# First attention stage of a two-block transformer on one core: compression branch threaded through the attention steps, twelve modulation steps moved beside weight panels, mask and score products in half-array pairs

## What is computed

```python
mod = jax.nn.silu(c) @ ada_w[i] + ada_b[i]            # six modulation vectors of 1024
h = rms_norm(x, attn_norm[i]) * (1.0 + sc_a) + sh_a
mq, mk, mv, nq, nkv, ng = jnp.split(h @ w_in, SPARSE_SPLITS, axis=-1)
o_moba = moba_attention(qk_prep(mq...), qk_prep(mk...), mv)
kc = nsa_compress(qk_prep(kv[0, 0]...), cmp_pos[0], cmp_w1[0], cmp_w2[0])
vc = nsa_compress(kv[0, 1], cmp_pos[1], cmp_w1[1], cmp_w2[1])
...
blocks = t[:, :, idx] + pos_emb                       # 15 blocks of 32 tokens, stride 16
hid = jax.nn.silu(jnp.einsum('bgnld,lde->bgne', blocks, w1))
return jnp.einsum('bgne,ed->bgnd', hid, w2)
...
o = g[..., 0:1] * o_c + g[..., 1:2] * o_s + g[..., 2:3] * o_w
```

## Time and profile before

| what | us |
|---|---|
| median of 3 runs | 1750.68 |
| the profiled execution, first to last instruction | 1748.3 |
| PE busy in it | 1575.0 (90%) |
| DVE busy | 940.4 (54%) |
| ACT busy | 718.2 (41%) |
| the three input panels, 45.4 to 112.9 | 67.5 |
| from the last panel to the first attention step, 112.9 to 197.6 | 84.6 |
| `attention(0)`, 197.6 to 261.0 | 63.4 |

### The profile page before, as it was taken

One profiled execution on the slowest core, in us unless ns is written; L12 is line 12 of the kernel. 1 busy time (PEld: TensorE's weight loads), 2 busy tenths in 40 slices (PEclk: granted clock), 3 DMA queues, 4 the chain that ended last, 5 costly groups with the idle time before them and its releaser, 6 DMA issues.

```text
span 1748.3 us, 24466 instructions
## 1 busy us (share of the span) xinstructions
PE 1575.0 (90%) x10302; PEld 1322.1 (76%) x10302; DVE 940.4 (54%) x1610; ACT 718.2 (41%) x1098; POOL 0.2 (0%) x4
## 2 busy tenths in 40 slices
PE   3966988999989888999988999889999795999997
PEld 1753677999868657999768998679987673779986
DVE  2591346434577776433566345663355786364455
ACT  1441244334445434333335554354544443345543
POOL 0000000000000000000000000000000000000000
PEclk9988798999989889999988999889999897989999
DMA  9844602985545546998753645549755353436452
GB/s 359 313 149 158 224 19 79 315 286 188 174 147 185 176 142 214 307 307 302 242 180 97 190 172 193 181 137 300 249 185 202 109 181 109 162 129 192 169 192 85
DMA packets 165845, 336.42 MB, mean 192 GB/s; under 512 B 8160, under 2 KB 109160, under 8 KB 165480
## 3 DMA queue, kind: packets, MB, share of 16 engines
q1 hardware_dynamic: 134720, 226.71, 38.0%
q10 hardware_dynamic: 31016, 108.16, 18.2%
HBM read 333.79 MB, written 1.05 MB: 192 GB/s over the span
## 4 chain that ended last, share of the span: by engine, by line
PE 80%; DVE 13%; DMA 2%; ACT 2%; issue 1%; ACTq 0%; SPq 0%; DVEq 0%
PE ps L1508 21%; PE ps L1509 21%; PE ps L1510 20%; PE ps L1480 5%; DVE wlo L903 3%; PE ps L1639 2%; DVE res L981 1%; DVE work L979 1%; PE ps L1636 1%; PE ps L1723 1%; PE ps L1673 1%; PE ps L1706 1%; DMA ring<-in_ada_w_dram 1%; PE ps L1702 1%; DVE work L1066 1%
## 5 line engine op out<-in xcount | busy, mean ns | idle before, releaser
L903 DVE TENSOR_TENSOR wlo<-wraw,whi 128x1024 fp32r<-128x1024 f32 (+1 forms) x424 | 497.9, 1216 | 404.4 <-ACT whi L526 403.9
L526 ACT ACTIVATE whi<-wraw 128x1024 fp32r<-128x1024 f32 (+1 forms) x424 | 423.1, 1045 | 468.7 <-PE ps L1510 447.0
L1508 PE MATMUL ps<-hT_hi,whi 128*128 128x256 f32 x1472 | 422.5, 287 | 0.0
L1509 PE MATMUL ps<-hT_lo,whi 128*128 128x256 f32 x1472 | 416.9, 283 | 0.0
L1510 PE MATMUL ps<-hT_hi,wlo 128*128 128x256 f32 x1472 | 416.5, 283 | 0.0
L1508 PEld LDWEIGHTS ps<-hT_hi,whi 128*128 128x128 f32 x1472 | 282.7, 192 | 20.3 <-issue 18.1
L1509 PEld LDWEIGHTS ps<-hT_lo,whi 128*128 128x128 f32 x1472 | 282.9, 192 | 0.0
L1510 PEld LDWEIGHTS ps<-hT_hi,wlo 128*128 128x128 f32 x1472 | 282.8, 192 | 0.0
L1508 PE MATMUL ps<-whi,act_hi 128*128 128x512 f32 x560 | 219.0, 391 | 0.0
L1509 PE MATMUL ps<-wlo,act_hi 128*128 128x512 f32 x560 | 218.1, 390 | 0.0
L1510 PE MATMUL ps<-whi,act_lo 128*128 128x512 f32 x560 | 217.9, 389 | 0.0
(11 more groups left out here) (200 smaller groups left out, 1372.1 us busy)
## 6 DMA issues: line engine op xcount, KB each, us to landing
wraw<-in_mlp_w_dram SPq DMA_DIRECT2D x96, 1024.0 KB, 5.3
ring<-in_ada_w_dram ACTq DMA_DIRECT2D x90, 1024.0 KB, 5.3
wraw<-in_ffn_w_gate_dram SPq DMA_DIRECT2D x22, 1024.0 KB, 6.4
wraw<-in_ffn_w_up_dram SPq DMA_DIRECT2D x22, 1024.0 KB, 5.6
wraw<-in_ffn_w_down_dram SPq DMA_DIRECT2D x22, 1024.0 KB, 4.9
wraw<-in_diff_w_in_dram SPq DMA_DIRECT2D x12, 1024.0 KB, 4.9
wraw<-in_attn_w_qkv_dram SPq DMA_DIRECT2D x12, 1024.0 KB, 5.1
wraw<-in_sp_w_in_dram SPq DMA_DIRECT2D x8, 1024.0 KB, 13.0
```

The lines of the kernel that those rows point to most:

```text
L526: nc.scalar.activation(whi[:, u % 2, part], wraw[:, u % 4, part], ACT.Copy).then_inc(hi_ready, 1)
L903: nc.vector.tensor_tensor(wlo[:, u % 2, part], wraw[:, u % 4, part], whi[:, u % 2, part].bitcast(F32), ALU.subtract).then_inc(lo_ready, 1)
L1508: mm(dst, s_hi, m_hi, start=start, stop=False, skip_group_check=skip)
L1509: mm(dst, s_hi, m_lo, start=False, stop=False, skip_group_check=skip)
```

## The change

- The panels are computed in the order `in0_2`, `in0_0`, `in0_1` (`IN0_ORDER`), each with `ada_step` beside all its units; `attention(0)` has no modulation steps now (`a.ada` 0) and `out0` has four. Norm and rotation of the NSA keys run beside `in0_0`, of the MoBA heads beside `in0_1`, of the NSA queries between the groups of `turns`. `turns(0)` is in parts, the groups with the compression keys first.
- The four units of `w1` leave the ring and pass through `wraw` between `in0_1` and `out0` (`compression_dma`); `out0`'s units wait for `cmp_used`. The first `w1` product alternates between its two column groups.
- The rest of the compression branch is placed in iterations 0 to 12 of `attention(0)` (`compression(i)` on PE, ACT and DVE), all of it in PSUM bank 7. The compressed rows are added instead of copied, and the first NSA heads write instead of adding.
- The splits of `out0`'s first two units are done in iterations 8 and 10 of `attention(0)`.
- `scores` in stages 0 and 1: the mask is two products of 64 rows per head, and the two heads alternate, instruction by instruction.
- `columns(0, 1)` comes after `out0`; on DVE it follows `residual`. The load of `ctx` moves from before `in0_1` to the eighth unit of `up0`.

```diff
-        for n, (a, b) in enumerate(((0, 1024), (1024, 2048), (2048, SP_IN))):
+        IN0_ORDER = (2, 0, 1)
+        IN0_SPAN = ((0, 1024), (1024, 2048), (2048, SP_IN))
+        for n in IN0_ORDER:
+            a, b = IN0_SPAN[n]
...
-            a.ada = {0: 4, 1: 8, 3: 8}[stage]
+            a.ada = {0: 0, 1: 8, 3: 8}[stage]
...
+            def compression_dma(j):
+                before = CMP_RAW + j - 4
+                sp.wait_ge(lo_ready, 2 * (before + 1))
+                slot = (CMP_RAW + j) % 4
+                dst = wraw[:, slot, :].rearrange("p (k e) -> p k e", k=8)
+                sp.dma_start(dst, w1c[j % 2][:, (j // 2) * 8:(j // 2 + 1) * 8, :]).then_inc(raw_full[slot], 16)
...
+            row_segment("in0_1", ada=True, heads=lambda i: heads0(0, (i,)), own=True)
+            nc.vector.memset(mark[:, 1:2], 0.0).then_inc(sem("moba_heads0"), 1)
+            panel_rows(r0, 1024, 1024)
+            turns(0, 0, 4)
...
+            nc.vector.memset(hidr[:, :], 0.0).then_inc(sem("hidr_zero"), 1)
+            nc.vector.memset(cmp_s, NEG)
+            heads0(1, (0, 1))
+            turns(0, 4, 6)
+            heads0(1, (2,))
+            turns(0, 6, 8)
+            heads0(1, (3,))
+            nc.vector.memset(mark[:, 1:2], 0.0).then_inc(sem("query_heads0"), 1)
...
+                if i == 3:
+                    dve.wait_ge(sem("cmp_vrep"), 1)
+                    nc.vector.tensor_tensor(vbd, ps[:, LINK_BANK, :], const("headmask"), ALU.mult).then_inc(sem("cmp_vbd"), 1)
...
+                if i in (10, 12):
+                    t = (i - 10) // 2
+                    dve.wait_ge(sem("cmp_pv"), t + 1)
+                    compressed_rows(t)
+                if i in (8, 10):
+                    split_unit(by_name["out0"]["base"] + (i - 8) // 2)
...
-                        mm(ps[:, bank, 0:256], ident_r[:, :], causal_r[:, :], start=True, stop=False, skip_group_check=True)
-                        mm(ps[:, bank, 0:128], q[:, 0:128], k[:, 0:128], start=False, stop=True, skip_group_check=True)
...
+                        for half in range(2):
+                            for m in range(2):
+                                lo, hi = HD * m, HD * m + HD
+                                bank = 2 * (i % 2) + m
+                                mm(ps[:, bank, 0:256], half_r[lo:hi, HD - HD * half:3 * HD - HD * half], causal_r[lo:hi, half, :, :].rearrange("p b n -> p (b n)"),
+                                   start=(half == 0), stop=False, skip_group_check=True)
+                        for tq, tk, at in ((0, 0, 0), (1, 1, 128), (1, 0, 256)):
+                            for m in range(2):
+                                q, k, _ = operands(i, m)
+                                bank = 2 * (i % 2) + m
+                                ins = mm(ps[:, bank, at:at + P], q[:, tq * P:(tq + 1) * P], k[:, tk * P:(tk + 1) * P], start=False, stop=True, skip_group_check=True)
...
-            ada_step()
-            pe.wait_ge(sem("cmp_silu"), 1)
...
+            attention(0, beside=compression)
+            pe.wait_ge(sem("cmp_taken"), 2)
+            out_turn(0)
+            row_segment("out0", ada=True)
             columns(0, 1, 6)
```

More of the change, by code:

```diff
@@ L1323, in _ @@
+            attention(0, beside=compression)
+            out_turn(0)
+            row_segment("out0", ada=True)
+            residual(0)
             columns(0, 1)
[L1324 to L1326 removed]
             norm()
@@ L1665, in gate, with turns @@
                     gate_out[0] = (gate_copied, 2 * sum(1 for g in GATES[:e + 1] if not (g[0] == 2 and g[2] == 0)))
-            def turns(stage):
-                for g, (srcs, _) in enumerate(q_groups(stage)):
+            def turns(stage, first=0, last=None):
+                groups = q_groups(stage)
+                last = len(groups) if last is None else last
+                for g in range(first, last):
+                    srcs, _ = groups[g]
                     if g >= 4:
```

453 lines of the change are left out of this document (245 added, 208 removed).

## The result

The changed kernel takes 1711.58 us (median of 4 runs, 1709.14 to 1715.86), the kernel before, run beside it, 1752.41. The ratio is 0.977, 95% interval 0.975 to 0.979. The forecast was 1702 with a range of 1690 to 1714. The profiled execution took 1709.3 us. Its span is 1707.2, against the span of 1748.3 from which the sum was made: -41.1 where the sum said -48.8. So the median is in the range and 9.6 us above the forecast, and one of the four executions, at 1715.86, is above the range. 7.7 of the 9.6 us are in the sum; the other 2 are that the median lies 4.4 above this span, where the forecast added 2.4. The 7.7 are not spread over the terms. They sit in one place, C, and A gives a part back.

A forecast was written before the change was run, and what follows sets the result against it. PE was taken to bound panels and attention, with no engine full in the 84.6 us between. Terms +9.2 - 63.0 + 2.6 - 1.1 + 5.0 - 1.5 = -48.8 on 1748.3 give 1699.5; median 2.4 above, 1702; range 1690 to 1714.

The forecast's parts named there:

- C: Attention stage: cheaper scores, added branch work and waits give 66.0 us against 63.4: +2.6, bounds -5 to +12.
- A: Panels: eight more modulation steps beside them, less a shorter first split and a wait: +9.2 us, bounds +8 to +14.
- B: Last panel to first attention step: the serial branch goes, DVE sets 21.6 us of 84.6: -63.0, bounds -64 to -58.
- plus 1.5 for a cold start: Attention stage: 1.5 us added to 64.5 for beginning at the low clock, giving 66.0.
- If the clock falls to the low level in mid attention: Attention stage: listed sign of a wrong forecast; it would double the 3.2 us of a step.
- D: Behind attention: the four `modrow` transposes move into PE's wait behind `out0`: -1.1 us.
- E: `out0`: it gets the four modulation steps that attention gave up: +5.0 us.
- F: `attention(1)`: DVE is the bound, so cheaper scores give at most 1.9 us; taken as -1.5.
- R1: Attention scores: loads of two row groups do not overlap: 1706 us, 1710 with the `w1` product serial too; chance 0.20.
- R2: Attention stage: the branch's links and two splits hold it longer than laid out: 1708 to 1720 us; chance 0.13.
- R3: Attention stage: the waits of 17.8 us overlap better, the stage takes 57: 1692 us; chance 0.04.
- R4: Scores: each row-group change drains the array; gain gone from 0.29 us a change, 1762 us at 0.35; chance 0.02.

The follow-up runs named there:

- e5_serial_w1: Changed kernel with the `w1` product going through its two column groups one after the other instead of alternating; 1708.0 us.
- e10_all_narrow: Changed kernel with `out0`'s splits late, `vcr` spread by wide products, and filler transposes nobody reads in PE's attention-stage waits; 1694.1 us.
- e9_pause_in_before: Kernel before the change, with PE made to wait once, in iteration 6 of `attention(0)`, for six extra DVE subtractions; 1776.0 us against 1751.2.
- e12_tail: e10_all_narrow plus filler transposes in its last two pauses, before the last values and before `out_turn`; 1689.4 us.
- e1_fill: Changed kernel with filler transposes nobody reads in front of PE's waits for copied probabilities, `vcr` and `vbd`; 1704.0 us against 1711.6.
- e4_by_head: Changed kernel with the scores of the two heads done one after the other instead of alternating, in both attention stages; 1723.5 us.
- e2_no_branch: Changed kernel with the compression branch left out of the attention stage, so the result lacks compressed attention; 1694.3 us.
- e8_by_head_no_branch: Changed kernel with the edits of e2_no_branch and e4_by_head together; 1706.5 us.
- e11_all_broad: Same as e10_all_narrow, but with one product of 256 columns as filler in place of each four transposes; 1695.0 us.

## Why the forecast was right, and what was off in it

- **A** was too dear by 3.7 us. The price of a step beside a unit held (6.68 and 5.53 us a period). The first split was put at -0.5; in fact the panels started 3.4 us earlier, about 2.8 of them the load that landed sooner and 0.7 the shorter split. The load rate of the narrow panel was put too high: its unit is 792 of 1024 columns, 0.81 MB, so with the ring unit 1.86 MB in 5.7 us are 326 GB/s and not 368, and no load stopped PE there.
- **B** held: 20.9 against 21.6, with DVE as the bound and the `w1` product beside it. The overlap of the column groups, taken from the modulation step, is shown by e5_serial_w1.
- **C** is the term that was mis-sized: +14.6 for +2.6. Not in the scores (1.10 us at the high level against 1.35), not in the waits (16.1 against 18.6), and not in the count of PE's work, which e10_all_narrow gives as 45.6 against 45.9. The step that failed is "plus 1.5 for a cold start". The forecast listed waits of 17.8 us in all, and costed each at its own length. The clock fell behind most of them and stayed low longer than they were: the scores behind the wait of 1.47 us and behind that of 2.85 still run at the low level. 61.9 us busy against 45.9 at the high level are 16.0 that this cost; 1.5 of them were foreseen, and the waits came out 2.5 shorter, which leaves the 12.0. "If the clock falls to the low level in mid attention" stood under what would prove the forecast wrong, without a price and without a chance. e9_pause_in_before shows such a price: 6 us of pause, 18 us behind it. That the low level is the loss is shown by that run and by e10_all_narrow. That pauses alone bring it about is shown for the 6 us pause and for the two at the end (e12_tail); for the links of the branch it is not, by the second fall in e1_fill.
- **D**: `columns` did move off the path, but `out_turn` got 0.8 us longer at the low level, so nothing shows at its old place; 0.8 us came back between `out0` and `up0`. **E**: +5.7 for +5.0, its first step cold, 1.94 instead of 1.07. **F** held.
- **R1** fell. Two row groups do load side by side: 0.063 us an instruction alternating, 0.84/7 = 0.12 one head at a time, both high. At the low level it is 0.12 alternating (1.41 us from 164.84 to 166.25 for 12) and 1.65/8 = 0.21 one at a time. So in one row group the price of an instruction with its load nearly doubles when the clock halves. The Trainium skill, page "TensorE: Matmul & The Clock Gate", section "LDWEIGHTS (loading the stationary operand)", gives a load its columns over 1.2 GHz and names no dependence on the clock; the low rows, and those of the earlier trace rows, disagree, and the measurement decides.
- **R2** named the right place with the wrong mechanism. The two splits cost 2.85 and 3.03 us of waiting, as laid out; moving them brought 7.5 us, since PE's busy time fell by 4.2 in the stage beside 2.1 of waiting. Its price was also added up wrong: six links at 1 to 2 us on top of 1702 are 1708 to 1714, not 1720. **R3**'s 57 us for the stage are near the 61 that a held clock gives, but not by its mechanism; the waits did not overlap better, they came to 16.1. **R4** fell: a change of row group costs nothing that the rows show.

The stated chances have two slips that change nothing else: the range 1690 to 1714 holds R3 too, which makes it 0.90, and the parts of R4 give 0.01 for slower.

That the time is in the range owes something to luck: A came out 3.7 us below its forecast and C 12.0 above. With A as forecast the time would have been 1715.3, above the range.

## What to carry to other kernels

When a dense stretch of TensorE is replaced by one with short pauses, cost the clock behind each pause and not only the pause; read the granted clock beside the idle time of the same windows. Where a pause can't be removed, cheap instructions of TensorE into a bank that is free can hold the clock: here they brought, with late splits and one wider product, 22 us of 1711. The clearest single case is the tail, where filling the last two pauses made the kernel 4.7 us faster. Move work that delays another engine's short chain (here a weight split ahead of the maxima) behind the last link of that chain.

## What the runs showed of the hardware that was not expected

- At 0.50 TensorE can stay there while it is busy: 38.88 of 38.90 us in e9_pause_in_before, 87.42 of 91.00 in e4_by_head. The same work, begun at 1.00, stayed at 1.00 for 50 us in the kernel before. What ends the low stretch stays open: the clock came back after 6.5 us (the changed kernel), 9 (e2_no_branch), about 30 (e8_by_head_no_branch), over 90 (e4_by_head) or not within the stage (e9_pause_in_before).
- Runs of one program differ with it: four runs of e4_by_head lie 17.8 us apart, with mean clocks of 0.927 to 0.939, and those of the changed kernel 6.7, with 0.942 in the fastest and 0.935 in the slowest; those of e10_all_narrow and e12_tail, whose clock is held, 2.3 and 3.2.
- With late splits and the wide product, f32 transposes as fillers kept the clock at 1.00 over 61 us (e12_tail). With wider products as fillers it was 0.96 over the stage (e11_all_broad, last pauses not filled) where transposes gave 0.99 (e10_all_narrow), and the times are the same.
